# Two pairs of small-product stages of the delta-rule inverse are merged: products of different row groups alternate in one stage

## The reference

```python
m = jnp.where(strict, jnp.einsum('bnhcd,bnhsd->bnhcs', k_beta, k) * decay, 0.0)
eye = jnp.broadcast_to(jnp.eye(c, dtype=f32), m.shape)
t_mat = lax.linalg.triangular_solve(m + eye, eye, left_side=True, lower=True,
                                    unit_diagonal=True)
u = jnp.einsum('bnhcs,bnhse->bnhce', t_mat, v_beta)
w = jnp.einsum('bnhcs,bnhsd->bnhcd', t_mat, k_beta * jnp.exp(gc)[..., None])
...
def step(state, inp):
    w_i, u_i, qd_i, kd_i, a_i, gl_i = inp
    v_new = u_i - jnp.einsum('bhcd,bhde->bhce', w_i, state)
    o_i = (jnp.einsum('bhcd,bhde->bhce', qd_i, state)
           + jnp.einsum('bhcs,bhse->bhce', a_i, v_new))
    state = state * gl_i[..., None, None] + jnp.einsum('bhcd,bhce->bhde', kd_i, v_new)
    return state, o_i
```

## Time and profile before

| | |
|---|---|
| median of 3 runs | 1269.85 us (1267.41 to 1270.79) |
| profiled execution | 1270.86 us, its span 1269.1 us |
| PE busy | 1205.5 us, 95% of the span |
| POOL, DVE, ACT busy | 880.4, 719.3, 705.6 us |
| the loop over n = 0 to 31 | about 142.5 to 245 us |

### The profile page before, as it was taken

How to read it: one execution, slowest core, us unless ns; L and a number is a source line. 1 busy time by engine, 2 the same in 40 slices (tenths; PEclk the granted TensorE clock), 3 DMA queues, 4 the chain that set the end, 5 groups by cost and what they waited for, 6 DMA issues and landing times.

```text
span 1269.1 us, 23466 instructions
## 1 busy us (share of the span) xinstructions
PE 1205.5 (95%) x8148; PEld 1087.5 (86%) x8148; DVE 719.3 (57%) x1514; ACT 705.6 (56%) x1318; POOL 880.4 (69%) x371
## 2 busy tenths in 40 slices
PE   8979899888899999899999999899999999999997
PEld 7978798877899999797999999788788887999996
DVE  4658657645576667565576666358245634444444
ACT  7756567645455555665555555665456544544442
POOL 5836633247598888644598888688778455988882
PEclk9989999999999999999999999999999999999999
DMA  7678532224766666523466666466556334665650
GB/s 280 187 135 168 146 99 84 67 84 150 211 202 191 189 195 187 155 92 100 123 204 190 192 187 194 140 198 187 169 161 229 103 129 135 185 196 182 183 164 34
DMA packets 61064, 203.27 MB, mean 160 GB/s; under 512 B 6320, under 2 KB 12720, under 8 KB 60864
## 3 DMA queue, kind: packets, MB, share of 16 engines
q1 hardware_dynamic: 53280, 192.96, 49.6%
q10 hardware_dynamic: 7712, 9.32, 3.7%
HBM read 198.07 MB, written 4.19 MB: 159 GB/s over the span
## 4 chain that ended last, share of the span: by engine, by line
PE 83%; DVE 7%; ACT 4%; issue 3%; POOL 1%; DMA 1%; ACTq 1%; SPq 0%; DVEq 0%; POOLq 0%
PE bank L180 20%; PE bank L181 19%; PE bank L182 19%; PE solve L182 5%; PE solve L181 5%; PE solve L180 5%; ACT whi L163 1%; DMA raw<-in_stream 1%; DVE xlo L309 1%; PE bank L827 1%; ACT xhi L303 1%; POOL wlo L167 1%; ACTq L1325 0%; PE bank L1681 0%; DVE area L712 0%
## 5 line engine op out<-in xcount | busy, mean ns | idle before, releaser
L167 POOL TENSOR_TENSOR wlo<-raw,whi 128x1024 fp32r<-128x1024 f32 x363 | 875.3, 2437 | 366.1 <-ACT whi L163 364.6
L163 ACT ACTIVATE whi<-raw 128x1024 fp32r<-128x1024 f32 x364 | 381.7, 1054 | 145.9 <-PE bank L182 129.8
L180 PE MATMUL bank<-xhi,whi 128*128 128x256 f32 x928 | 271.4, 292 | 15.8 <-DVE xlo L309 9.8
L182 PE MATMUL bank<-xhi,wlo 128*128 128x256 f32 x928 | 265.5, 286 | 0.0
L181 PE MATMUL bank<-xlo,whi 128*128 128x256 f32 x928 | 265.5, 286 | 0.0
L180 PEld LDWEIGHTS bank<-xhi,whi 128*128 128x128 f32 x928 | 180.8, 195 | 21.2 <-DVE xlo L309 10.6
L180 PE MATMUL bank<-whi,xhi 128*128 128x512 f32 (+2 forms) x456 | 179.3, 393 | 7.5 <-issue 4.4
L181 PEld LDWEIGHTS bank<-xlo,whi 128*128 128x128 f32 x928 | 181.0, 195 | 1.1
L182 PEld LDWEIGHTS bank<-xhi,wlo 128*128 128x128 f32 x928 | 180.8, 195 | 0.0
L182 PE MATMUL bank<-whi,xlo 128*128 128x512 f32 (+2 forms) x456 | 175.4, 385 | 0.0
L181 PE MATMUL bank<-wlo,xhi 128*128 128x512 f32 (+2 forms) x456 | 175.1, 384 | 0.0
(11 more groups left out here) (414 smaller groups left out, 1735.9 us busy)
## 6 DMA issues: line engine op xcount, KB each, us to landing
raw<-in_stream SPq DMA_DIRECT2D x364, 512.0 KB, 3.6
band_scratch<-band ACTq DMA_DIRECT2D x1, 3072.0 KB, 35.8
area<-band_scratch ACTq DMA_DIRECT2D x2, 1024.0 KB, 12.5
resid<-in_x SPq DMA_DIRECT2D x2, 512.0 KB, 6.3
scr<-in_row_b_gate ACTq DMA_DIRECT2D x1, 1024.0 KB, 4.7
out<-resid SPq DMA_DIRECT2D x4, 256.0 KB, 2.0
tab<-in_tabs ACTq DMA_DIRECT2D x1, 640.0 KB, 10.6
area<-in_row_final ACTq DMA_DIRECT2D x1, 512.0 KB, 5.1
```

The costliest lines, as they stand in the source:

```text
L163: act.activation(whi[:, n.s, :], raw[:, n.s, :], ACT.Copy).then_inc(hi_ready, 1)
L167: pool.tensor_tensor(wlo[:, n.s, :], raw[:, n.s, :], whi[:, n.s, :].bitcast(F32), ALU.subtract).then_inc(lo_ready, 1)
L180: nc.tensor.matmul(out_ap, a_hi, b_hi, start=start, stop=False)
L182: return nc.tensor.matmul(out_ap, a_lo, b_hi, start=False, stop=stop)
```

## The change

The products of `i = 1` move into the stage `i = 0`, where they alternate with those already there, and the products of `i = 3` into the stage `i = 2`, between the two of each pair. The stages `i = 1` and `i = 3` are gone. ACT makes its two copies in one place, and DVE its three. The number of products, their operands and the number of copies stay the same.

```diff
--- before.py
+++ after.py
@@ -1015,24 +1015,17 @@
                         pe.wait_ge(DN.solved, 1)
                         pe.wait_ge(DN.z_silu, 8)
                     for j, m in enumerate(ms):
-                        mm = pe.matmul(bank[32:64, j * 32:j * 32 + 32], MU[0:32, m, 32:64], TN[0:32, m, 0:32], start=True, stop=True)
-                if i == 1:
-                    pe.wait_ge(DN.tile_copied, 7 * q + 1)
-                    for j, m in enumerate(ms):
-                        mm = pe.matmul(bank[96:128, j * 32:j * 32 + 32], MU[64:96, m, 96:128], TN[64:96, m, 0:32],
-                                       start=True, stop=True)
+                        c = slice(j * 32, j * 32 + 32)
+                        pe.matmul(bank[32:64, c], MU[0:32, m, 32:64], TN[0:32, m, 0:32], start=True, stop=True)
+                        mm = pe.matmul(bank[96:128, c], MU[64:96, m, 96:128], TN[64:96, m, 0:32], start=True, stop=True)
                 if i == 2:
                     pe.wait_ge(DN.tile_copied, 7 * q + 2)
                     pe.wait_ge(DN.spread, 5)
                     for j, m in enumerate(ms):
-                        c, p = slice(256 + j * 32, 288 + j * 32), PM[32:64, j * 32:j * 32 + 32]
+                        c, p, p3 = slice(256 + j * 32, 288 + j * 32), PM[32:64, j * 32:j * 32 + 32], PM[96:128, j * 32:j * 32 + 32]
                         pe.matmul(bank[32:64, c], MU[32:64, m, 32:64], p, start=True, stop=True)
+                        pe.matmul(bank[64:96, c], p3, MU[96:128, m, 96:128], start=True, stop=True)
                         mm = pe.matmul(bank[0:32, c], p, MU[32:64, m, 32:64], start=True, stop=True)
-                if i == 3:
-                    pe.wait_ge(DN.tile_copied, 7 * q + 4)
-                    for j, m in enumerate(ms):
-                        c, p = slice(256 + j * 32, 288 + j * 32), PM[96:128, j * 32:j * 32 + 32]
-                        mm = pe.matmul(bank[64:96, c], p, MU[96:128, m, 96:128], start=True, stop=True)
                 if i == 5:
                     pe.wait_ge(DN.tile_copied, 7 * q + 5)
                     for j, m in enumerate(ms):
@@ -1114,7 +1107,7 @@
                     if g is not None:
                         stage(g)
                 q, i = tile_at(n)
-                if i in (0, 1, 2, 3, 5, 7):
+                if i in (0, 2, 5, 7):
                     tiles(q, i)
             tokens_still(pe, unit(BASE["wout"] + 15), ACC, [slot_of(15)], 512, xhi, xlo, False, True, True, RS.bank)
 
@@ -1173,11 +1166,11 @@
                                scale=colv("out_norm")).then_inc(DN.hi, 1)
 
             def tile_copy(q, i):
-                act.wait_ge(DN.tile, 6 * q + (0, 1, 2, 3, 0, 4, 0, 5)[i] + 1)
-                if i < 2:
+                act.wait_ge(DN.tile, 4 * q + (1, 3)[i == 5])
+                if i == 0:
                     act.wait_ge(DN.spread, 5)
-                    own = slice(32 + 64 * i, 64 + 64 * i)
-                    act.activation(PM[own, 0:256], ps[0][own, 0:256], ACT.Copy).then_inc(DN.tile_copied, 1)
+                    for own in (slice(32, 64), slice(96, 128)):
+                        act.activation(PM[own, 0:256], ps[0][own, 0:256], ACT.Copy).then_inc(DN.tile_copied, 1)
                 else:
                     act.activation(PM[64:128, :], ps[0][64:128, :], ACT.Copy).then_inc(DN.tile_copied, 1)
 
@@ -1193,7 +1186,7 @@
                 if n == 33:
                     copy_v(7)
                 q, i = tile_at(n)
-                if i in (0, 1, 5):
+                if i in (0, 5):
                     tile_copy(q, i)
                 if n % 2 == 0 and 2 <= n <= 32:
                     conv_finish(act, 16 + c - 1)
@@ -1263,7 +1256,7 @@
                                          ALU.mult, ALU.subtract).then_inc(DN.lo, 1)
 
             def tile_copy(q, i):
-                dve.wait_ge(DN.tile, 6 * q + (0, 1, 2, 3, 0, 4, 0, 5)[i] + 1)
+                dve.wait_ge(DN.tile, 4 * q + (2, 4)[i == 7])
                 ms = slice(8 * q, 8 * q + 8)
 
                 def copy(dst, rows, cols, n):
@@ -1273,7 +1266,6 @@
                 if i == 2:
                     copy(TN[32:64, ms, 0:32], slice(32, 64), slice(256, 512), 32)
                     copy(MU[0:32, ms, 32:64], slice(0, 32), slice(256, 512), 32)
-                elif i == 3:
                     copy(MU[64:96, ms, 96:128], slice(64, 96), slice(256, 512), 32)
                 else:
                     copy(MU[0:64, ms, 64:128], slice(0, 64), slice(0, 512), 64)
@@ -1286,7 +1278,7 @@
                     if g is not None:
                         stage(g)
                 q, i = tile_at(n)
-                if i in (2, 3, 7):
+                if i in (2, 7):
                     tile_copy(q, i)
                 if n % 2 and n < 32:
                     conv_taps(dve, 16 + n // 2)
```

## The result

| | before | after |
|---|---|---|
| median | 1269.15 us (4 runs, 1267.41 to 1270.79) | 1260.74 us (4 runs, 1259.12 to 1265.17) |
| profiled execution | 1270.86 us, span 1269.1 | 1265.17 us, span 1263.3 |
| the loop, from the first stage 0 to the first product behind it | 100.17 us | 94.66 us |

The ratio is 0.9939 [0.9911, 0.9968]: the change makes the kernel faster, by 8.4 us between these medians and by 5.7 us between the profiled executions (1270.86 and 1265.17).

The account below looks back on a forecast made before the run. PE, busy 95% of the span, was taken to bound the kernel. Quarter gains of 2.15, 1.45, 0.94 and 0.94 us sum to 5.5, giving 1264.4 us against the median of the runs shown; range 1261.5 to 1268.0.

Parts of the forecast that it names:

- Stages 1 and 3 cost PE 0.78 us each: In each quarter of the loop, removing either stage saves PE 0.78 us if its products ride along for nothing.
- Alternating row groups cost nothing: In merged stages 0 and 2, products of different rows and columns overlap like column pairs; lower bound of the cost nothing.
- Rivals 1 (row groups take turns): In both merged stages, products of different rows writing one bank run one after the other: 1267.3 us, chance 0.2.
- 2 (a drain at each change): In both merged stages, each row-group change costs some 0.16 us, 19.8 us over 124 changes: 1281 us, chance 0.06.
- The third product of a round: In stage 2, 16 more records add 0.1 us; upper bound, with nothing overlapping, 1.0 us.
- First quarter: Stage 2 starts 3.23 us sooner, half clock costs 1.33 us, and `v_turn` comes 2.15 us sooner.
- The half clock behind it: In the first quarter the clock falls again, so the half unit behind stage 2 takes 2.78 us, paying 1.33 us.
- Third and fourth quarter: The 1.11 us wait for DVE's copies goes, about 1.6 us for `second_values` comes; 0.94 us gained in each.
- rival 3: In the third and fourth quarters the new 1.6 us waits lower the clock: 2.8 us gained, 1267.0 us, chance 0.1.
- Sum: Over the loop's four quarters, 2.15 + 1.45 + 0.94 + 0.94 = 5.5 us gained, which stays gained behind the loop.
- The step that failed is the last: For the whole kernel, 1265.4 us from the profiled execution, set 1.0 lower to the shown runs' median: 1264.4 us.
- rival 4: ACT and DVE chains looser, up to 7.4 us gained, 1262.4 us, or tighter, 4.5 us gained; chance 0.09.

Follow-up runs that it names:

- the late copy: Changed kernel with three loads on SP's queue and DVE's third copy put back behind the scaling, at `i = 3`: median 1258.69 us, ratio 0.991 of the kernel before.

## Why the prediction was right in its parts and wrong in its level

- **Stages 1 and 3 cost PE 0.78 us each, with cover for what rides along: right.** In the second quarter, where no wait interferes, 1.58 was gained of 2 x 0.78 = 1.56.
- **Alternating row groups cost nothing: right**, and it was the step without a row. Stage 0 takes 0.62 with 32 records, and grouping the same products takes 1.02. Rivals 1 (row groups take turns) and 2 (a drain at each change) fall with it. The Trainium skill's rule (TensorEngine Tiling (Array Packing), Gotcha 1: PSUM Pressure) is not borne out for f32 products of 32x32 with outputs in different partitions: starts lie 0.00 to 0.01 us apart into one bank, and 32 records take the time of 16. The prediction's 0.62 / 16 = 0.04 between records of one position takes in the change-over; the distance itself is 0.03. Row groups that write the same partitions were not tried.
- **The third product of a round: 0.1 forecast, 0.01 measured** (1.17 against 1.16).
- **First quarter: 2.15 forecast, 2.42 measured.** Stage 2 came 151.40 - 145.22 = 6.18 behind stage 0, as forecast (151.30 - 145.12). The half clock behind it came as forecast too, 2.73 us for the half unit against 2.78. What was mis-sized is the stage itself, 0.85 and 0.1, from the row of line 1022, which ran as the clock fell; it took 152.07 - 151.40 = 0.67. From the half unit's end to `v_turn` were 3.23 us, forecast 3.22. But the term holds only for this length of the half clock. It was 3.4 us in the two profiles compared; with 6.8 in both (before and changed kernel, loads moved), it is 24.50 - 21.84 = 2.66.
- **Third and fourth quarter: 0.94 forecast, 0.76 and 0.75 measured.** The wait for DVE's copies went, and one for `second_values` came, 1.53 (forecast 1.6); the clock didn't fall behind it, so rival 3 is out. The scaling came 199.54 - 189.24 = 10.30 behind stage 0, before 203.55 - 193.14 = 10.41: 0.11 sooner, not 0.19. That is 0.1 of the difference. The other 0.1 lies behind the wait: from `second_out` to the next half unit are 202.41 - 201.06 = 1.35, and before, entered without a wait, 1.24. That this is the entry out of idle was only read, not tried.
- **Sum: 5.5 forecast, 5.51 in the loop.** Span to span it is 5.8.
- **The step that failed is the last**: "The median of the runs shown lies 1.0 below it; against that the sum gives 1264.4 us", with "some scatter of the runs" in a range of 1261.5 to 1268.0. It put a sum that holds to a tenth on a level taken from three runs. Three executions between 1267.4 and 1270.8 looked like a scatter of 3 us; the 78 of the three groups go from 1259.2 to 1277.8, with medians of 1267.5, 1268.1 and 1269.7. With a standard deviation of 3 to 4 a median of three or four executions is uncertain by about 2 us, on either side of the comparison. The low end came from rival 4's price (1262.4) with 0.9 us for that. The 78 have a mean of 1268.4; less 5.5 that is 1262.9, and the changed kernel's 16 have a mean of 1262.0. So of the 3.7 us between 1264.4 and the measured 1260.74, 1.5 are the level of the kernel before, and the rest is how low the changed kernel's own four executions lay.
- **What the level is made of** was in the trace of before, outside what the prediction read. The profiles are alike to a few tenths of a us over most of the program, and differ where the clock is at half in some executions and not in others, for 3.4 us in most places: ahead of the loop (0 to 3 times), in the first quarter, twice, once or not at all at a cost between the loop and the first MLP (67.3, 65.7 or 64.1 us), around the start of the second MLP (none or once, 1.5 us), and between 802 and 817 us (3.4 or 6.8 us long, 1.2 us apart). In the first quarter 3.4 and 6.8 us of it are 24.50 - 23.09 = 1.4 apart before and 21.84 - 20.67 = 1.2 after. The other part is ACT's issuing of loads, which costs PE 0 to 3.3 us and at times half clock behind it: the stretch is 193.63 to 193.65 us in the five profiles with the loads moved and 194.0 to 199.0 in the eight others. That part was shown by moving the loads; that of the clock was read, and only the first quarter's was tried.
- **The times follow the clock in all executions**, not only in the profiled ones. Each has its mean granted clock on record: in the 78 of the kernel before it goes from 0.995 (1259.2 us) to 0.981 (1277.8 us), with a correlation of -0.93, and 0.001 of it comes with 1.15 us. Compared at the same granted clock by such a line, an estimate, the changed kernel (16 executions) is 5.3 us below the kernel before (78; standard error 0.4) and, with the loads moved, 6.0 us below (standard error 0.5), where the loop gained 5.5 and 5.7 and the bare means of the second pair differ by 8.4. The loads are worth 2.7 us and the late copy 1.3 (standard error 0.5 each), so its 1.2 us of loop are there.
- **Can the gain lie above 5.5?** The timed differences of 8.4 (4 runs each), 5.4 and 8.4 shrink to about the loop's when the clock is taken out, as far as it is on record, and no stretch behind the loop is regularly shorter in the profiles. Whether the change also makes half clock elsewhere rarer stays open: the mean granted clock is 0.9886 against 0.9878, and 0.9893 against 0.9871 with the loads moved, differences of one and a half and of two standard errors.

## What to carry to other kernels

Small independent products of different row and column positions can alternate in one stage at the price of one position, even into one PSUM bank, so pair stages whose operands are ready together, and check on DVE and ACT which chain the bundled copies now stand ahead of; splitting such a bundle again can give back part of it. Before a forecast of half a per cent, look for waits in the whole program that could differ from execution to execution (a long issue, a low clock behind a wait), and give a median of three runs its own uncertainty in the range. Where each execution's granted clock is on record, compare executions of like clock: here that took most of the scatter away (1.4 us were left of 3.7).

## What the runs showed that was not expected

- Where a wait of 2.1 to 3.5 us had brought the half clock, it lasted 3.4, 6.8 or 10.2 us, for the same wait: 2.42 us was followed by 3.4 us in two profiles and by 6.8 in another, 2.43 by 10.2. Why it differs stays open.
- A wait of 1.53 us at `second_out`, with 128x128 records behind it, left the clock at 1.00. One of 1.18 us at `v_turn`, with four 128x128 and sixteen 64x64 records behind it, was followed by half clock, in both profiles that have it.
- The issue of one transfer held ACT between 2.06 and 4.8 us for the second bias load and between 4.66 and 6.4 us for the broadcast of the positions, with the same instructions each time. What lengthens it wasn't tried.
